# One subtraction per weight slab instead of two, behind the modulation units, in a two-layer decoder trunk

## The reference

```python
c_act = silu(c)
for l in range(2):
    mod = c_act @ ada_w[l] + ada_b[l]                 # 2048 x 6144 weights for one row
    shift, scl, gate_res = split(mod, 3)
    h = rms(x, norm_g[l]) * (1 + scl) + shift
    z = h @ (ev_w_in if l == 0 else od_w_in)          # slabs 0..47, and 64..124
    # layer 0: u, q, k, v, g: causal pooling beside attention
    # layer 1: q, k, v, indexer, ga, gb, g: sparse attention beside a 31-tap convolution
    y = concat(branches)
    x = x + gate_res * ((y * silu(g)) @ w_out[l])     # slabs 48..63, and 125..140
```

## Time and profile before

| | |
|---|---|
| Median of 3 runs | 1017.18 us (1017.04 to 1020.48) |
| The profiled execution | 1017.85 us |
| Its span in the trace | 1016.1 us |
| Mean granted clock of TensorE | 0.985 |
| Instructions | 20238 |
| Read from HBM | 256.07 MB |

### The profile page before, as it was taken

The page is one execution under the profiler, slowest core; times in us unless marked ns, Lnnn a source line. Parts: engine busy times, 40 slices in busy tenths (PEclk is TensorE's granted clock), DMA queues, the critical chain, the costliest instruction groups (busy, mean ns, idle before and its releaser), DMA issues.

```text
span 1016.1 us, 20238 instructions
## 1 busy us (share of the span) xinstructions
PE 955.8 (94%) x7728; PEld 945.8 (93%) x7728; DVE 835.2 (82%) x1244; ACT 437.3 (43%) x693; POOL 46.7 (5%) x63
## 2 busy tenths in 40 slices
PE   5197799999999999999999999999999999999997
PEld 5197789999999999999999999999999999999997
DVE  4898987987899778887877898888999986878842
ACT  4122125434555444333344444444446555743331
POOL 1000000011010000000000000000010100000000
PEclk9997798999999999999999999999999999999999
DMA  8999988989777888899857755544445555588961
GB/s 337 339 325 360 324 296 316 321 287 369 290 275 243 279 285 287 312 359 362 312 189 269 242 196 180 189 137 162 150 162 180 167 172 199 196 309 307 342 220 41
DMA packets 71094, 261.32 MB, mean 257 GB/s; under 512 B 7904, under 2 KB 8032, under 8 KB 70768
## 3 DMA queue, kind: packets, MB, share of 16 engines
q1 hardware_dynamic: 68544, 250.86, 70.0%
q0 software_dynamic: 2480, 9.50, 2.6%
HBM read 256.07 MB, written 4.19 MB: 256 GB/s over the span
## 4 chain that ended last, share of the span: by engine, by line
PE 77%; DVE 14%; DMA 4%; issue 3%; ACT 2%; SPq 0%; DVEq 0%; POOL 0%; ACTq 0%; POOLq 0%
PE bank L707 20%; PE bank L708 19%; PE bank L709 19%; DVE acc L1038 6%; DVE wlo L1027 3%; PE bank L809 3%; DMA ada<-ada_units 3%; PE bank L812 3%; PE bank L811 3%; PE bank L724 1%; PE bank L726 1%; PE bank L727 1%; PE bank L777 1%; DVE X L1105 1%; ACT whi L400 1%
## 5 line engine op out<-in xcount | busy, mean ns | idle before, releaser
L400 ACT ACTIVATE whi<-raw 128x1024 fp32r<-128x1024 f32 x282 | 297.2, 1060 | 447.6 <-PE bank L709 338.5
L1027 DVE TENSOR_TENSOR wlo<-raw,whi 128x1024 fp32r<-128x1024 f32 x282 | 341.4, 1224 | 91.9 <-ACT whi L400 91.3
L707 PE MATMUL bank<-hhi,whi 128*128 128x256 f32 x1168 | 337.1, 289 | 2.3 <-ACT T L619 0.9
L708 PE MATMUL bank<-hlo,whi 128*128 128x256 f32 x1168 | 330.4, 283 | 0.0
L709 PE MATMUL bank<-hhi,wlo 128*128 128x256 f32 x1168 | 330.3, 283 | 0.0
L1038 DVE SCALAR_TENSOR_TENSOR acc<-ada,cact,acc 128x1024 f32<-128x1024 f32 x176 | 226.1, 1285 | 33.0 <-DMA ada<-ada_units 16.5
L707 PEld LDWEIGHTS bank<-hhi,whi 128*128 128x128 f32 x1168 | 223.9, 192 | 5.7 <-issue 3.8
L708 PEld LDWEIGHTS bank<-hlo,whi 128*128 128x128 f32 x1168 | 224.1, 192 | 0.1
L709 PEld LDWEIGHTS bank<-hhi,wlo 128*128 128x128 f32 x1168 | 223.8, 192 | 0.0
L707 PE MATMUL bank<-ghi,whi 128*128 128x256 f32 x512 | 147.9, 289 | 0.0
L708 PE MATMUL bank<-glo,whi 128*128 128x256 f32 x512 | 144.9, 283 | 0.0
(11 more groups left out here) (166 smaller groups left out, 1070.1 us busy)
## 6 DMA issues: line engine op xcount, KB each, us to landing
raw<-w_slabs SPq DMA_DIRECT2D x282, 512.0 KB, 4.9
ada<-ada_units SPq DMA_DIRECT2D x192, 512.0 KB, 6.3
X<-xT SPq DMA_DIRECT2D x1, 2048.0 KB, 7.6
x_dram<-X POOLq DMA_DIRECT2D x4, 512.0 KB, 5.4
outT<-X POOLq DMA_DIRECT2D x4, 512.0 KB, 5.0
V<-pool_w POOLq DMA_DIRECT2D x1, 1024.0 KB, 6.2
U<-xT POOLq DMA_DIRECT2D x2, 512.0 KB, 9.8
V<-xT POOLq DMA_DIRECT2D x2, 512.0 KB, 7.4
```

Of the source, the lines that this page charges most:

```text
L400: act.activation(whi[:, slot], raw[:, slot], ACT.Copy).then_inc(hi_done, 1)
L707: mm(out, whi[:, s, k, :], ahi[:, c, :], start=(c == 0), stop=False)
L708: mm(out, whi[:, s, k, :], alo[:, c, :], start=False, stop=False)
L1027: dve.tensor_tensor(wlo[:, s], raw[:, s], whi[:, s].bitcast(F32), ALU.subtract)\
```

## The change

`lo` subtracts a whole slab in one instruction over 2048 columns. It waits for the copies of both halves and counts `lo_done` up by two at its end. The calls for the first half, which stood at the head of a step, are gone; the call for the whole slab stands where the second half was, behind the step's units. In step 62 the call for the first half of slab 65 is gone too, and the whole slab comes behind the first four chunks of h. ScalarE's copies, SP's loads and their waits, and TensorE's work are not changed.

```diff
-            def lo(w, t, halves=(0, 1)):
-                for half in halves:
-                    s = half_slot(w, half)
-                    dve.wait_ge(hi_done, 2 * now(w, t) + half + 1)
-                    dve.tensor_tensor(wlo[:, s], raw[:, s], whi[:, s].bitcast(F32), ALU.subtract)\
-                        .then_inc(lo_done, 1)
+            def lo(w, t):
+                s = half_slot(w, 0)
+                dve.wait_ge(hi_done, 2 * now(w, t) + 2)
+                dve.tensor_tensor(wlo[:, s:s + 2], raw[:, s:s + 2], whi[:, s:s + 2].bitcast(F32), ALU.subtract)\
+                    .then_inc(lo_done, 2)
...
             def plain(w, t):
-                lo(w + AHEAD, t, (0,))
                 units(w, t)
-                lo(w + AHEAD, t, (1,))
+                lo(w + AHEAD, t)
...
             def attention_step(w, v0, g0, layer, more=None):
                 i = w - v0 - 3
-                lo(w + AHEAD, None, (0,))
                 divide(layer, i - 1)
...
                 units(w, None)
-                lo(w + AHEAD, None, (1,))
+                lo(w + AHEAD, None)
...
                 def step(w, t):
-                    last = w + AHEAD >= N_SLABS
-                    if not last:
-                        lo(w + AHEAD, t, (0,))
                     units(w, t)
                     add_x(w, t, o0, layer)
-                    if not last:
-                        lo(w + AHEAD, t, (1,))
+                    if w + AHEAD < N_SLABS:
+                        lo(w + AHEAD, t)
                 return step
...
             step_o(O0, 0)(62, None)
-            lo(65, None, (0,))
             for g in range(3):
                 make_gain(1, g)
             add_x(63, None, O0, 0)
...
             make_h(1, range(0, 4))
-            lo(65, None, (1,))
+            lo(65, None)
             units(63, None)
```

## The result

| | before | after | ratio |
|---|---|---|---|
| Median, first comparison | 1018.05 us (4 executions) | 1041.13 us (4 executions, 1037.18 to 1045.2) | 1.0223 [1.0165, 1.0282] |
| Median, the same two compared again | 1017.14 us (21) | 1040.14 us (5, 1036.99 to 1043.79) | 1.0225 [1.0203, 1.0246] |
| Profiled execution | 1017.85 us, span 1016.1 | 1037.23 us, span 1035.4 | |

The change makes the kernel slower by 23 us, 2.2%. "Before" and "after" stand for the two kernels. The profiled execution is one of the short ones: 19.4 us above that of before.

A forecast was written before the change was run, and what follows sets the result against it. TensorE, 94% busy, was taken as the bound, losing time only where it waits. Terms 2.8 + 1.6 + 8.2 + 2.6 + 2 + 1 + 0.9 - 0.3 = 18.8 us on the 1017.18 median gave 1036 us, range 1023 to 1045.

The forecast's parts named there:

- the four places: Start, slab 26, change of layers and output stages, where later subtractions were to delay TensorE; with the clock, chance 0.55.
- the rival with the unit loads: Output stages: unit loads set 13.2 us for two steps, +5 and +5 in place of 3: 1043 us, chance 0.13.
- Instruction: All slabs: one subtraction of 2048 columns takes 2.30 us, holding VectorE 2.22 us instead of 2.27.
- Start: To 152.8 us: slabs 2, 5 and 8 lose 1.07 us each waiting for second copies, eight others return 0.4: +2.8.
- Slab 26: Whole subtraction, behind reciprocal roots and two units, ends at 263.13 us where TensorE opened at 261.52: +1.6 us.
- Change of layers: Slabs 65 to 73: copy, subtraction, load and h form one chain, its delays adding to +8.2 us (4 to 9.5).
- TensorE's clock: Ahead of slab 73: TensorE idles some 3 us and its granted clock falls: +2.6 us, other end 0.
- Output stages: Two-step loop of loads, units, addition, subtraction takes 12.4 to 13.2 us: first stage +1, last +2 (each 0 to 5).
- Attention: Attention steps: division of probabilities no longer stands behind a first half; -0.3 us, low end -6.1.
- the rival: Attention, slabs 28 to 36 and 106 to 114: line 844's 6.1 us of TensorE idle time go: 1011 us, chance 0.03.
- Small terms: Gated low parts at slabs 48 and 125, and slab 103 behind the second roots: +0.9 us together.
- The rule: VectorE: grouping helps a saturated engine; otherwise smaller pieces finish sooner. First half gave about 1009; second keeps the slowdown.

The follow-up runs named there:

- experiment 7: Experiment 6 with two subtractions, each waiting for its own copy, for slabs 2, 5 and 8: 1020.76 us, ratio 1.0025.
- experiment 6: After with SP issuing the unit loads ahead of the raw slab in every step: 1024.13 us, ratio 1.0071.
- experiment 3: After with the old order and two instructions (first half, units, addition to x, second half) in both output stages alone: 1029.85 us, ratio 1.0103.
- experiment 4: After with SP issuing units ahead of the raw slab in the output stages alone (steps 48 to 61, 125 to 131): 1030.61 us, ratio 1.0123.
- experiment 5: After with two instructions at the change of layers alone (slabs 65 to 73), slab 65's first half at its old place: 1034.41 us, ratio 1.0158.
- experiment 1: After with the old two instructions, each waiting for its own copy, at the new places behind the units: 1021.23 us, ratio 1.0042.
- experiment 9: Experiment 6 with halves for slabs 2, 5, 8, 26, 103 and the change of layers, one instruction for 127 slabs: 1015.32 us, ratio 0.9987.
- experiment 10: Experiment 1 with SP issuing the unit loads ahead of the raw slab in all steps: 1015.44 us, ratio 0.998.
- experiment 11: The kernel before with SP issuing the unit loads ahead of the raw slab in every step: 1020.2 us, ratio 1.0028.
- experiment 2: After with two instructions for the one, both waiting for the second copy: 1036.32 us, ratio 1.018.

## Why the prediction was right, and where it was not

The side and the four places were right, and the size was near: +18.8 forecast (1036), +23 by the medians (1041.1 and 1040.1), inside the range, +19.4 in the trace. Both medians lie nearer to the 1043 of the rival with the unit loads than to 1036, and that the sum of 18.8 met the 19.4 of the trace so closely was luck: errors of over 7 us cancel in it.

- **Instruction.** 2.30 us forecast, 2288 ns. VectorE 12.1 us less busy; nothing came of it where TensorE sets the pace.
- **Start.** +2.8 forecast; 3.4 by the medians of experiment 7 against 6 (4.7 by the ratios, within 2.8). In the trace of after only +1.1 at chunk 14 and +0.1 behind it. Five traces with the same start (after, its repeat, and experiments 3, 4, 5) lag +1.1, +1.5, +5.3, +3.5 and +4.6 at chunk 14, 3.2 on average; five traces in which these slabs have two instructions with a wait each (experiments 1, 7, 9, 10 and 11) lag from -0.8 to +1.8, 0.1 on average. The step held; one trace would not have shown it.
- **Slab 26.** +1.6 forecast, 1.75. The subtraction ended at 263.25 against 263.13 forecast and TensorE opened at 263.39:

```profile
260.96 2.29 DVE L1026 TENSOR_TENSOR wlo<-raw,whi 128x2048 fp32r<-128x2048 f32 x1
...
263.39 0.36 PE L809 MATMUL bank<-whi,hhi 128*128 128x256 f32 x1 [1.59 <-DVE wlo L1026]
```

- **Change of layers.** +8.2 forecast, 7.1, of which 0.8 is the last of the output stage; from chunk 0 of h on it is 6.2. Taking off the 8.59 us by which chunk 0 is late, slab 66 was done at 531.96 (forecast 531.9) and chunk 4 was 1.6 late (1.4). The unit load left at 532.84 (532.8), but took 5.38 us, not 7.1. So the unit was late by 0.7 instead of 2.4, chunk 8 by 2.8 instead of 4.3, the end of slab 70 by 2.4 instead of 4.9. The step that failed is one latency: I took the nearest row, 7.1, which was too long here. (At slab 73 the working's own 6.3 + 2.0 is 8.3, not 8.2.)
- **TensorE's clock.** +2.6 forecast (the row named gives 2.9: 37 matmuls in 7.0 us, where they take 4.1 afterwards), 0 found in both traces of after. TensorE idled 3.3 us of the 4.5 ahead of slab 73, and the granted clock stayed at the level of 2.4 GHz. At chunk 14, after 2.1 us of idling in the 4 us ahead of it, the clock was down, as before. The stretch behind the first pause, the one with the second, and the one behind that (columns as in the earlier trace rows):

```profile
154.00:159.80 5.80, 5.80 (x36) 5.80 (x37) 4.29 (x4) 3.58 (x4) 0.00 (x0) 0.71 0.83 287
...
584.90:589.40 4.50, 1.20 (x11) 1.00 (x9) 2.84 (x4) 4.17 (x6) 0.00 (x0) 1.00 0.00 1
589.40:594.00 4.60, 4.60 (x38) 4.60 (x39) 4.60 (x8) 0.43 (x1) 0.00 (x0) 1.00 0.69 224
```

  In 154 to 159.8 it did 36 matmuls in 5.8 us, in 589.4 to 594 it did 38 in 4.6. But the term was not empty. In experiments 2, 3 and 4, whose change of layers has the same order and waits for the second copy as in after, TensorE waited 2.97, 2.28 and 2.18 us ahead of slab 73, and there the granted clock did fall, to 0.50 for 2 to 3 us; slab 73 took 7.34 us in place of 5.86. So the fall occurred in three of five such traces and cost 1.5 us, and 2.6 was its price at chunk 14, not here. The first 2 us of slab 73 in experiment 4:

```profile
584.44:586.44 2.00, 2.00 (x9) 2.00 (x10) 2.00 (x1) 0.00 (x0) 0.00 (x0) 0.50 0.47 90
```
- **Output stages.** +1 and +2 forecast, +6.0 and +4.3 found. The loop was the right mechanism and was even written down as a rival with 13.2 us a turn, +5 and +5, at a chance of 0.13; its price came true. Two things failed. The latency was the median of the whole span, 6.3 us, while the unit loads of after have a median of 7.3 from 428 to 519 us and of 7.1 from 925 to 975, and the chain shows 6.14 to 7.80 in the last stage and 8.70 in the first, with a 512 KB store of GpSimd issued beside it at 439.72. The trace of before, asked for these stages alone (428 to 519 and 915 to 968 us), already had 6.8 and 7.3. And I let the first stage's 6.3 us a slab pass for reserve, though the loop of two steps there came to 13.7 us, 6.84 a slab.

```profile
438.14 8.70 DMA ada<-ada_units
...
448.75 2.21 DVE wlo L1026
```

- **Attention.** -0.3 forecast, -0.6 and -0.7 found, -1.3 together. The idle time of line 844 went from 6.1 us to the row below, so the rival had a true core and a fraction of its price.

```profile
  DVE SP L1221: 3.5, 7
```

- **Small terms.** +0.9 forecast, +1.4 found (0.5, 0.4, 0.4 at slabs 48, 103, 125).
- **The rule.** Of the two halves of what the Trainium skill (Perfetto Trace Analysis, Optimizing Scalar/DVE Operations) says, the second decided. At 79 to 82% busy, VectorE had nothing to gain from the longer instruction. But smaller pieces alone do not finish work sooner: with one wait for both copies they took 1036.3 us (experiment 2), with a wait each 1021.2 (experiment 1).

Together: output stages, slab 26 and small terms 7.9 us too low; start, clock, change of layers and attention 7.4 us too high in this trace. The medians lie 4 us above it.

What stays open is that spread: after runs from 1037 to 1045 us, before from 1017 to 1020.5 in the same comparison. Part of it goes with the clock: the two executions of 1045 us had a mean granted clock of 0.982, the two of 1037 us 0.987 and 0.985. By that, an estimate is that 3 to 5 of the 8 us are lost to the lower level, (0.987 - 0.982) x 1035 and (0.985 - 0.982) x 1037; at which pauses, no trace shows. Another place where it can come from is slab 23: in before TensorE had 3.2 us of reserve there, in the trace of after 0.15. In experiment 3's long execution one unit load took 12.98 us there, and the chain passes through it:

```profile
231.12 12.98 DMA ada<-ada_units
...
245.52 2.29 DVE wlo L1026
...
247.95 0.35 PE bank L707
```

That it is the same in after's long executions is argued, not shown.

## What to carry to other kernels

An instruction joined from two waits for the last of its inputs and releases at the end of all of them. Its cost isn't its own duration but what stands behind it: price each load that is queued behind a load that its end releases, and follow the circle once round with the latency of that stage, not of the whole span. If the circle is longer than the pace of the bounding engine, either split the instruction, with a wait for each part, or reorder the queue: here the order on SP gave back some 16 of 23 us, the split at 14 slabs the rest. And an engine that is 80% busy and waits for its input gains nothing from 127 fewer instructions (experiment 9).

## What the runs showed of the hardware that I had not expected

- The granted clock after a pause isn't repeatable. At chunk 14 of h, after 2.1 us of idling in the 4 us or so ahead, the next 36 matmuls took 6.83 us in before, 5.78 in after, and 4.29 in experiments 1 and 10, where the clock had stayed up. Ahead of slab 73 it did not fall in after, with a wait of 3.30 us, and did fall in experiments 2, 3 and 4, with waits of 2.97, 2.28 and 2.18 us.
- A 512 KB unit load took from 5.4 to 13.0 us on the path: 5.38 at 541 us, 6.14 and 7.80 in the last stage, 8.70 at 438, 12.98 at 231 us in experiment 3, with two 512 KB loads of GpSimd passing. That the traffic beside them makes the difference is likely, but was not varied by itself.
